# Gates and projections of three mixer branches laid into the attention stages of a decoder step

## What is computed

```
h = rms_norm(x, n1);  z = h @ w_in                      # all mixers' inputs
o_gla, o_hgrn, o_pool = gated linear attention, HGRN2, causal pooling (z)
o_nsa = compressed + selected (top 16 blocks of 64) + window attention (z, paged caches)
proj  = einsum('blnc,ncd->blnd', [o_gla, o_hgrn, o_pool, o_nsa], w_branch)   # 4 x (512 -> 1024)
gate  = sigmoid(h @ w_gate + b_gate)                    # 4 x (1024 -> 1024)
x = x + sum_b(gate_b * proj_b) @ w_out
x = x + relu(rms_norm(x, n2) @ w1)**2 @ w2
```

## Time and profile before

| | us |
|---|---|
| median of 3 runs | 1506.16 (1505.02 to 1507.02) |
| profiled execution | 1503.8 |
| its span, first to last instruction | 1502.0 |
| mean granted TensorE clock | 0.922 of 2.4 GHz |
| PE busy | 1298.2 (86%) |
| POOL / DVE / ACT busy | 542.9 / 568.0 / 403.9 |
| moved by DMA | 139.15 MB, mean 93 GB/s |

### The profile page before, as it was taken

The page is one execution under the profiler, slowest core; times in us unless marked ns, Lnnn a source line. Parts: engine busy times, 40 slices in busy tenths (PEclk is TensorE's granted clock), DMA queues, the critical chain, the costliest instruction groups (busy, mean ns, idle before and its releaser), DMA issues.

```text
span 1502.0 us, 24320 instructions
## 1 busy us (share of the span) xinstructions
PE 1298.2 (86%) x10284; PEld 1220.6 (81%) x10284; DVE 568.0 (38%) x800; ACT 403.9 (27%) x605; POOL 542.9 (36%) x262
## 2 busy tenths in 40 slices
PE   4698998998974477786489999997979999999998
PEld 3598997897863355565389999997969999999998
DVE  3433664261435776764571111112133410134102
ACT  3342212013450123222152322233232211122210
POOL 2335432054129900025033434343324434344341
PEclk9799999999985698898679999999989999999999
DMA  4221001532145510038113232322212322323222
GB/s 160 99 72 56 29 29 57 125 104 79 32 174 218 208 73 1 1 117 332 57 43 99 84 98 84 98 85 83 71 50 91 93 90 85 94 87 96 86 86 83
DMA packets 43585, 139.15 MB, mean 93 GB/s; under 512 B 3975, under 2 KB 15595, under 8 KB 42107
## 3 DMA queue, kind: packets, MB, share of 16 engines
q1 hardware_dynamic: 37762, 104.70, 21.9%
q0 software_dynamic: 5760, 33.56, 6.1%
HBM read 129.97 MB, written 8.49 MB: 92 GB/s over the span
## 4 chain that ended last, share of the span: by engine, by line
PE 76%; DVE 13%; issue 3%; DMA 3%; ACT 2%; POOL 1%; DVEq 0%; ACTq 0%
PE PS L555 53%; PE PS L583 7%; PE PS L635 3%; DVE tmp L1309 2%; DMA M<-cache_slc_kv,idx 2%; PE PS L874 1%; PE PS L888 1%; PE PS L924 1%; DMA M<-weights 1%; DVE hL L1313 1%; DVE M L1714 1%; PE PS L861 1%; PE PS L773 1%; PE PS L726 1%; PE PS L670 1%
## 5 line engine op out<-in xcount | busy, mean ns | idle before, releaser
L1879 POOL TENSOR_TENSOR WL<-M,WH 128x1024 fp32r<-128x1024 f32 x159 | 386.7, 2435 | 693.3 <-ACT WH L1051 693.1
L555 PE MATMUL PS<-hH,WH 128*128 128x260 f32 x1424 | 298.1, 291 | 30.3 <-DVE hL L1313 27.4
L1051 ACT CAST WH<-M 128x1024 fp32r<-128x1024 f32 x159 | 166.2, 1049 | 505.0 <-DMA M<-weights 505.0
L555 PE MATMUL PS<-hL,WH 128*128 128x260 f32 x1424 | 293.2, 288 | 0.0
L555 PE MATMUL PS<-hH,WL 128*128 128x260 f32 x1424 | 292.9, 288 | 0.0
L555 PEld LDWEIGHTS PS<-hH,WH 128*128 128x128 f32 x1424 | 226.2, 194 | 36.6 <-DVE hL L1313 14.0
L555 PEld LDWEIGHTS PS<-hL,WH 128*128 128x128 f32 x1424 | 226.2, 194 | 0.0
L555 PEld LDWEIGHTS PS<-hH,WL 128*128 128x128 f32 x1424 | 226.1, 194 | 0.0
L555 PE MATMUL PS<-uH,WH 128*128 128x260 f32 x512 | 103.2, 283 | 2.4 <-ACT M L1291 2.4
L555 PE MATMUL PS<-uH,WL 128*128 128x260 f32 x512 | 103.2, 283 | 0.0
L555 PE MATMUL PS<-uL,WH 128*128 128x260 f32 x512 | 103.0, 283 | 0.0
(11 more groups left out here) (347 smaller groups left out, 2008.8 us busy)
## 6 DMA issues: line engine op xcount, KB each, us to landing
M<-weights SPq DMA_DIRECT2D x159, 512.0 KB, 3.5
M<-cache_win_kv SPq DMA_DIRECT2D x2, 2048.0 KB, 7.9
spill<-xT SPq DMA_DIRECT2D x1, 2080.0 KB, 10.2
xT<-spill SPq DMA_DIRECT2D x1, 2080.0 KB, 8.8
M<-x_prompt SPq DMA_DIRECT2D x4, 512.0 KB
y_prompt<-M SPq DMA_DIRECT2D x4, 512.0 KB
con<-tables SPq DMA_DIRECT2D x1, 1437.5 KB, 12.4
M<-state_gla SPq DMA_DIRECT2D x2, 512.0 KB, 6.1
```

The costliest lines, as they stand in the source:

```text
L555: last = mm(PS[:, bank + h, 0:HALF], w[:, n % 4, k, :], x[:, HALF * h:HALF * h + HALF], start=(start and k == k0 and w is WH and x is hi), ...
L1051: nc.scalar.copy(WH[:, n % 4].rearrange("p k n -> p (k n)"), WR[:, n % 4]).then_inc(sem("w_hi"), 1)
L1879: p.tensor_tensor(WL[:, n % 4].rearrange("p k n -> p (k n)"), WR[:, n % 4], WH[:, n % 4].rearrange("p k n -> p (k n)"), ALU.subtract).then ...
```

## The change

- **Order of the mix.** Branches pooling, GLA, HGRN2 (`ORDER`) have their 12 chunks each (8 gate, 4 projection) in 96 half-steps of 260 columns: per pair of output tiles `m`, four gate halves, then four projection halves. 32 steps are laid into the preparation (PSUM banks 6 and 7 in turn), 48 into the prompt loop (bank 7 alone, three per two pairs), 16 into the decode attention (banks 6 and 7). Only NSA's 12 chunks stay behind the attention, as whole units.
- **Activations kept.** `hH`, `hL` aren't overwritten by the attention's scratch (which moves into free parts of other buffers), so `norm_apply("n3")` goes; x is read back into `x2` during the last mix part, and `w_out`'s result is added to it there.
- **Gates by tanh.** sigmoid(y) = (1 + tanh(y/2))/2: ACT does a tanh with bias and scale halved, DVE `(tanh + 1) * proj` in one instruction, and the factor 0.5 comes in with the final add.
- **Slots.** In the 36 chunks of the three branches only three weight slots are used; slot 3 of `WH` and of `WR` serve as two buffers (`W3`) of 1024 columns for the gathers.
- **Small pieces.** The compressed cache comes in 32 gathers of 512 KB, one quarter of a sample's rows each, summed by adds of 512, 256 and (but for the first of a sample) 256 columns. In POOL's queue they are mixed with `lower`: two, one, one pieces before the chunks of a group of three for the first twelve chunks, then three before each chunk until all 32 are done.
- **Ring.** The decode caches, window parts too (8 pieces now from POOL's queue), come as 40 pieces of 512 KB into a ring of ten buffers, in part free only late.
- The compressed steps in the loop sit four later (shift sums at u = 24, 26, 32, 34); transposed probabilities use one PSUM bank instead of two; four index columns per sample replace one.

The core of the diff (of POOL's queue, PE's, ACT's and DVE's steps):

```diff
+def slot_of(n):
+    return n % 4 if n < N_MIX else n % 3 if n < N_LAST else (n - N_LAST) % 4
...
+            def mix_step(k):                                   # PE
+                bi, m, t, h, gate, n = MIX[k]
+                if h == 0 and (gate or t == 0):
+                    pe.wait_ge(sem("w_lo"), n + 1)
+                earlier = [e for e in range(k) if mix_bank(e) == mix_bank(k)]
+                if earlier:
+                    pe.wait_ge(sem(mix_evac(earlier[-1])[0]), mix_evac(earlier[-1])[1])
+                if not gate and t + h == 0 and m == 0:
+                    pe.wait_ge(sem("b_lo"), bi + 1)
...
+                last.then_inc(sem("prod"), 1)
...
                 for c in range(2):
                     if 1 <= p < NP + 1:
                         probs_transposed(p - 1, c)
+                    if p < NP and 3 * p // 2 + c < 3 * (p + 1) // 2:
+                        mix_step(PREP + 3 * p // 2 + c)
                     if p >= 2:
                         probs_values(p - 2, c)
...
             def keys_transposed(j):
+                pe.wait_ge(sem(f"xq{j % 3}"), 64 * (j // 3 + 1))
...
+                    if s == 1:
+                        mix_step(PREP + LOOP + j + min(max(j - 1, 0), 6))
...
+            def mix_step(k):                                   # ACT
...
+                if gate:
+                    act.wait_ge(sem("prod"), units_before(N_MIX) + k + 1)
...
+                    f(SG[t][:, half], PS[:, mix_bank(k), 0:HALF], ACT.Tanh, bias=bgh[:, col:col + 1], scale=0.5)\
+                        .then_inc(sem("sg"), 1)
...
+                s = 4 * (not gate) + 2 * t + h
+                if s in (2, 4, 6):
+                    upper(N_MIX + 12 * bi + 3 * m + 1 + s // 2)
...
+                    out = GP[:, half] if bi else mixT[:, 2 * m + t, half]     # DVE
+                    v.scalar_tensor_tensor(out, SG[t][:, half], 1.0, PS[:, mix_bank(k), 0:HALF], ALU.add, ALU.mult)\
+                        .then_inc(sem("mix_mul"), 1)
...
+            compressed_gather(0)                               # POOL
+            compressed_gather(1)
+            lower(N_MIX)
+            lower(N_MIX + 1)
+            q = 0
+            for n in range(N_MIX + 2, N_MIX + 22):
+                for _ in range((2, 1, 1)[n % 3] if n < N_MIX + 12 else 3):
+                    if q < len(CPIECES):
+                        compressed_sum(q)
+                        q += 1
+                lower(n)
...
+                if n == 6:                                     # cache_piece(n), the ring
+                    gp.wait_ge(sem("on"), 2 * TT)
+                if n >= 10 and n % 4 == 2:
+                    gp.wait_ge(sem("oq_mm"), (n - 10) // 4 + 1)
...
-            dve.wait_ge(sem("xt_back"), 16)
-            norm_apply("n3", "n1")
```

More of the change, by code:

```diff
@@ L490, in _ @@
                          tail[HIST:HIST + NS]).then_inc(sem("stored"), 16)
-            sp.wait_ge(sem("pd"), 8)
-            sp.dma_start(SPARE, A["spill"]).then_inc(sem("xt_back"), 16)
+            for n in range(N_MIX, N_MIX + 3):
+                reload(n)
             sp.wait_ge(*done("k_norm"))
@@ L745, in _, with mix_steps @@
                     units(1)
+            def mix_step(k):
[7 more added lines that the diff above has]
+                    pe.wait_ge(sem("b_lo"), bi + 1)
+                half = slice(HALF * h, HALF * h + HALF)
+                for c in range(KT if gate else 4):
+                    hi, lo = hk(c) if gate else (bX[:, c], bL[ORDER[bi]][:, c])
+                    at = c if gate else 4 * t + c
+                    for w, x in ((WH, hi), (WH, lo), (WL, hi)):
+                        last = mm(PS[:, mix_bank(k), 0:HALF], w[:, slot_of(n), at, :], x[:, half],
+                                  start=(c == 0 and w is WH and x is hi), stop=(c == (KT if gate else 4) - 1 and w is WL))
+                last.then_inc(sem("prod"), 1)
+            def mix_steps(a, b):
+                for k in range(a, b):
+                    mix_step(k)
             pe.wait_ge(sem("hn_ln"), len(HN))
@@ L991, in _ @@
-            pe.wait_ge(sem("mix_mul"), 34)
+            pe.wait_ge(sem("oq_ev"), NJ)
+            pe.wait_ge(sem("b_lo"), 4)
+            for m in range(4):
+                if m:
+                    last_gate(m, 0)
+                    last_gate(m, 1)
+                last_proj(m, 0)
+                last_proj(m, 1)
+            pe.wait_ge(sem("sg"), 56)
+            pe.wait_ge(sem("mix_mul"), 55)
             for n in range(8):
                 pe.wait_ge(sem("w_lo"), N_OUT + n + 1)
+                if n == 1:
+                    pe.wait_ge(sem("mix_mul"), 56)
@@ L1194, in _ @@
             f(rk, rk, ACT.Exp, scale=-0.5).then_inc(once("rk"), 1)
-            act.wait_ge(*done("kst"))
-            step(f(kst[:, 0:2], kst[:, 0:2], ACT.Ln, bias=eps[0:32], scale=1.0 / HD))
-            f(kst[:, 0:2], kst[:, 0:2], ACT.Exp, scale=-0.5).then_inc(once("kst_rs"), 1)
+            upper(N_MIX + 1)
+            for k in range(9):
+                mix_step(k)
             act.wait_ge(*done("cm"))
             f(CM, CM, ACT.Exp).then_inc(once("cm_e"), 1)
+            for k in range(9, PREP):
+                mix_step(k)
             def compressed_step(u):
-                if u == 35:
+                if u == 39:
                     act.wait_ge(*done("kst_x"))
@@ new lines, in _ @@
+            for n in range(2):
+                cache_piece(n)
+            for n in range(N_MIX + 22, N_MIX + 31):
+                lower(n)
+            for n in range(2, 10):
+                cache_piece(n)
+            for n in range(10, 4 * NJ):
+                if n % 4 == 2 and N_MIX + 31 + n // 4 - 2 < N_LAST:
+                    lower(N_MIX + 31 + n // 4 - 2)
+                cache_piece(n)
+            lower(N_LAST)
+            lower(N_LAST + 1)
+            lower(N_LAST + 2)
+            lower(N_LAST + 3)
@@ L2017 @@
     gate = tiles(a["w_gate"][0]).reshape(4, 8, 128, KT, COLS)
-    branch = [tiles(a["w_branch"][0].reshape(2, 1024, 1024)[i]) for i in range(2)]
-    mix = np.stack([gate[0], gate[1], branch[0], gate[2], gate[3], branch[1]], 1).reshape(48, 128, KT, COLS)
+    branch = [a["w_branch"][0, b].reshape(4, 128, 4, 2, COLS).transpose(2, 1, 3, 0, 4).reshape(4, 128, KT, COLS)
+              for b in range(4)]
+    mix = np.concatenate([np.stack([gate[b, 0::2], gate[b, 1::2], branch[b]], 1).reshape(12, 128, KT, COLS)
+                          for b in (2, 0, 1, 3)])
     w1, w2 = a["mlp_w1"][0], a["mlp_w2"][0]
```

681 lines of the change are left out of this document (390 added, 291 removed).

## The result

| | before | after |
|---|---|---|
| median, us | 1506.59 (1505.02 to 1507.21) | 1548.36 (1541.96 to 1550.64) |
| ratio, 95% interval | | 1.027 (1.024 to 1.030) |
| span of the profiled execution | 1502.0 | 1547.4 |

The forecast was 1477, with 1430 to 1520 as its range: wrong in sign, by 71 us. Medians of the changed kernels are of four or five executions; of `c_ring_pace`, one slow execution (2457 us) is left out. Lines from here on are those of the kernel after; its half-step of the mix is L790, POOL's chunk subtraction L2043, the key transposes L987.

A forecast was written before the change was run, and what follows sets the result against it. PE, busy 86% of the span, was taken as the bound, with idle, slow-clock stages to fill. Rebuilt stages put the output product at 1020.5 instead of 1049.2, 29 us less: span 1473, execution 1475, median 1477; range 1430 to 1520.

The forecast's parts named there:

- Preparation: Stage before the prompt loop: POOL's sums and chunk subtractions set the pace, so the loop starts at 548 us, against 509.
- the tanh held behind the compressed scores: Preparation, between third and twelfth chunk: ACT's next tanh waits for the compressed keys' score matmuls, charged 7 us.
- Prompt loop: Loop carrying 48 half-steps: POOL bounds it first, some 41 us of new PE idle, then PE; it ends at 790 us.
- The nineteenth chunk: Prompt loop: POOL, at 14.7 us per chunk, finishes the chunk that pair 11 needs at 637 us.
- The slow clock: Decode attention: transposes after each exposed gap run at 3.68 instead of 1.97 us, 2.3 us each, 18 us.
- Decode attention: Ten jobs with 16 half-steps: 77 us of PE work, gather waits, slow clock and hand-offs, 148 us, ending at 944.
- Eight round trips: Decode attention, jobs 2 to 9: the ten-piece ring exposes a full gather wait of 5.8 us each, 46 us.
- End of the stage and the last branch: Merges and gate units take 18 us where 30.2 stood; the last branch's remaining work then reaches the output product at 1020.5.
- The sum: Whole kernel: output product at 1020.5 instead of 1049.2 us, a gain of 29 us, giving a median of 1477.
- both new bounds, POOL and ring: POOL's chunk period of 14.7 us in the early loop, and gather round trips of 46 us in the decode attention.

The follow-up runs named there:

- c_ring_pace: Changed kernel with a ring of twelve buffers, two compressed sums before the first chunk and two pieces, not three, before each loop chunk: 1480.1 us, ratio 0.984.
- i1: c_ring_pace with the upper half of the sixth mix chunk moved earlier in ACT's queue, after half-step 8: 1470.8 us, ratio 0.977.
- g0: Changed kernel with a ring of twelve buffers and the compressed sums' adds left out, so it computes less: 1443.2 us, ratio 0.956.
- e1: Changed kernel with a ring of twelve buffers instead of ten, lower chunk halves behind each job's gathers: 1498.7 us, ratio 0.996.
- h1: Changed kernel, ring still ten, with chunk subtractions 32 to 35 behind a job's four gathers instead of ahead: 1553.5 us, ratio 1.029.
- f1: c_ring_pace with the 16 half-steps of the decode attention run behind its last values: 1489.6 us, ratio 0.990.
- f2: f1 with 32 half-steps in the prompt loop instead of 48, and three sums again before each chunk: 1498.2 us, ratio 0.993.
- g1: Changed kernel with a ring of twelve buffers and all compressed sums made by DVE instead of POOL: 1522.8 us, ratio 1.010.
- g2: Changed kernel with a ring of twelve; DVE sums 16 of 32 compressed pieces in the preparation, POOL the rest: 1475.2 us, ratio 0.978.
- i2: g2 with the upper half of the sixth mix chunk moved earlier in ACT's queue, after half-step 8: 1468.0 us, ratio 0.973.

## Why the prediction was wrong, by its own steps

| stage | forecast | measured |
|---|---|---|
| loop starts | 548 | 566.2 |
| prompt loop | 242 | 283.2 |
| decode with its start | 154 | 166.8 |
| to the first projection of the last branch | 18 | 22.0 |
| to the output product | 58.5 | 58.0 |

- **Preparation, 18 us short.** The first three chunks were through at 446.3, 455.7 and 469.4 for 443, 454 and 464, so 5 us were lost by the third. The twelfth was through at 559.5 instead of 542. For the stretch between I charged 7 us for the tanh held behind the compressed scores; POOL stood for 13.9 there, and 8.0 more before two later chunks, 15 over the charge (its pieces and chunks took 2 to 3 less). i1 shows that this one upper half is worth 6 us of the start; why the other chunks came late is not taken apart.
- **Prompt loop, 41 us short: the step that failed.** Its busy time was 227.8 us against 193. I priced the 48 half-steps and the pairs at full clock and left out what a piece pays for standing alone; at 0.88 the half-steps alone took 128 instead of 103. By the granted clock over PE's busy time (0.89), an estimate, 25 of the 35 us are the clock. Its idle time came near the forecast only in sum, by luck: 55.4 us against 49, but 29.9 of them behind POOL where I had 41, and 25.5 in short hops where I had 8. The nineteenth chunk was late too (651.5, forecast 637); PE had stood for the eighteenth until 646.4 and was at pair 8, not 11. With POOL out of the way the loop still takes 250 us (g0): 217.6 busy, and 33 us of idle time where I allowed 8: 5.4 still behind POOL, the rest in short hops, the largest part (10.1 us in 7) before the transposes of probabilities.
- **The slow clock.** I gave the laid-in work none, and the decode attention 18 us. The half-steps take 56 us more than in the old stretch, some 36 of them for the 370 matmuls at 1.2 GHz. The rows from 633.78 on show the low level behind a wait of 6.83 us, and with POOL's waits gone (g0) the 370 are 231.
- **Decode attention: right in mechanism, sized 13 us too low.** Eight round trips were exposed, 57.7 us for the forecast 46, because the wait was 6.6 to 9.6 us instead of 5.8. That is 12 of the 13. e1 shows the cause, h1 that the order isn't one.
- **End of the stage and the last branch: right** within 4 and 1 us. The rest behind the output product is unchanged (451 us).
- **The sum.** 18 + 41 + 13 + 4 is 76; the output product starts at 1096 and not at 1020.5. The forecast saw both new bounds, POOL and ring, and then subtracted them from a gain counted at full clock. The right reading of the earlier trace rows was at hand: in these stages the clock stood at 0.59, 0.84 and 0.83, and what moves there from a stretch at 0.99 is priced by that clock until something shows that it rises. It became 0.84, 0.88 and 0.80.

## What to carry to other kernels

Work moved from a dense stage into a gappy one must be priced at the clock of the stage that it goes to; here a half-step laid into the loop or the decode attention was worth 0.6 us at most against one run behind them (f1, f2). When a change takes buffers from a ring, count how many jobs the rest holds: with ten pieces for jobs of four, every job from the third on paid a full round trip, and two more buffers, found in tables already used up, brought 50 us. Give a filler a queue order in which no engine waits for what it holds up itself.

## What the runs showed of the hardware

- A 260-column matmul takes 0.119 or 0.217 us from start to start, and 370 of the 1728 laid in (21%) ran at or near the lower level although PE was busy for three quarters of these stages (435.7 of 579.2 us).
- A half-step put ahead of the wait instead of between the transposes (h2) took 10.8 us off eight waits and under 5 off the total; the sixteen transposes behind each wait then took up to 3.87 us instead of 1.97 + 1.04.
- A DVE add of 512 columns, 0.68 us alone, takes 1.4 to 2.7 when it begins beside POOL's subtraction of 1024 columns; in all twelve such meetings of g1, g2 and i2 it ended 0.54 to 0.56 us behind the subtraction.
